# Expert weights in 2 MB pieces with 16 KB rows, and one more buffer for the first pair of experts, in a decoder block on one core

## The chip, the cores and the metric

The kernel runs on one core of a Trainium2 chip. The metric is the device time of one execution in microseconds (us); lower is better. The engines are named as the profile names them: PE is TensorE (PEld its weight loads), DVE is VectorE, ACT is ScalarE, POOL is GpSimd, SP is SyncE. SPq and ACTq are the queues in which SP and ACT issue DMAs.

## What is computed

One decoder block on 256 tokens of width 1024, all in float32. A mixer part (retention and pooling, merged by gates) comes first; then 32 experts, of which each token uses 4; then a per-layer embedding and a last norm. The change is about the experts:

```python
def swiglu_clamped(gu):
    gate, up = gu[..., :D_FF], gu[..., D_FF:]
    gate = jnp.minimum(gate, SWIGLU_LIMIT)
    up = jnp.clip(up, -SWIGLU_LIMIT, SWIGLU_LIMIT)
    return (up + 1.0) * (gate * jax.nn.sigmoid(gate * SWIGLU_ALPHA))
...
logits = xt @ w_router + b_router              # top 4 of 32, softmax over the 4
act = swiglu_clamped(xblk @ w_gate_up[e] + b_gate_up[e])   # w_gate_up[e]: 1024 x 2048
y  += slot_w * (act @ w_down[e] + b_down[e])               # w_down[e]: 1024 x 1024
```

Each expert has 8 MB of gate and up weights and 4 MB of down weights, 384 MB for the 32. All experts are computed, for up to 64 tokens each; more tokens for one expert would take an extra path (`more_pairs`), which is not entered for these inputs.

## The kernel before

**Stages.** The mixer (`column_block`, `project` and what surrounds them, L587 to L712) multiplies with weights split in a high and a low part: ACT writes w_hi (L957), DVE writes w_lo (L1201). Then come the router (L723 to L741), sixteen pairs of experts (`pair_steps` on PE, L850, and on DVE, L1435), the per-layer gate (L908 to L912) and the store (L507 to L511).

**A pair.** Two experts run side by side in TensorE: each takes 64 of its 128 columns, so a matmul of one expert lies beside that of the other. `gather` (L744) multiplies the normalised tokens xn, as stationary operand, with a one-hot matrix; DVE scales the result by the norm's gain into hg (`read_gather`, L1405). `up_bias` (L567) puts the biases in PSUM. `gate_up` (L765) goes through 8 blocks of 128 weight rows, with 4 column blocks of 512 for each expert. DVE clamps (L1413, L1414), ACT takes the sigmoid (L1075), DVE multiplies (L1418, L1422), and `act_to_width` (L774) transposes the result on TensorE (L780). `down` (L783) multiplies with w_down, and `scatter` (L802) adds the output to the tokens' rows, through DVE (L1433). In between TensorE does the previous pair's scatter and the next pair's gather. Pair 8 has extra work (`route_rest`, `project_ple`, `output_bias`, L811 to L848), which uses w_proj, 1 MB, loaded by ACT (L1048) before the first pair.

**The weights' way.** SP issues every weight load on one queue, in an order written out by hand (L453 to L484). Weights lie in a ring of 12 slots of 1 MB (8 KB for each of 128 partitions). A gate and up piece is one block of 128 rows of one expert: each partition gets one row, 8 KB in a piece. A down piece is two blocks of 128 rows: each partition gets two rows of 4 KB that lie 512 KB apart in memory. Pieces alternate between the two experts, so a pair has 24. A slot is free once the last matmul that reads it has counted up `used` (L762), and SP waits for that before each load (L483). TensorE waits for a piece of both experts before it starts on a block (`expert_ready`, L364). In gather and gate_up, row k*128 + p of a weight matrix goes with partition p of block k, and so does element k*128 + p of a token.

**Before the first pair.** The ring's upper six slots hold w_hi and w_lo of the mixer until its end: w_hi in slots 6 to 8, w_lo in 9 to 11. Loads of pair 0 start while the mixer still runs, into slots as they come free (`load_early`, L446) and into five buffers that the mixer has left (`extra_places`, L330), so 17 pieces can be there before TensorE starts on the pair. These five buffers are used once.

**Order on the other queues.** ACT issues the two bias rows of the next pair (`load_bias`, L1051), 8 KB each, into one partition each. DVE and ACT follow TensorE by semaphores that count (`chunk_used`, `gate_ready`, `act_ready`). At the start SP loads x, the norm gains and the positions (L407 to L412); TensorE transposes gains and positions (L581, L583), DVE copies them (L1187, L1188), and the first scaled columns of x wait for that.

The wait that the ring works by:

```python
with sp.Fori(1, PAIRS) as pair:
    for c in range(PER_PAIR):
        sp.wait_ge(used, PER_PAIR * pair + c - SLOTS + 1)
        load_expert(first, pair, c, 2 * pair + c % 2)
```

## Time and profile before

| | |
|---|---|
| median of 3 runs | 1279.01 us (1278.15 to 1279.05) |
| profiled execution, first to last instruction (span) | 1279.1 us |
| mean granted TensorE clock of that execution | 0.969 |
| TensorE, weight loads, DVE, ACT, POOL busy | 94%, 47%, 30%, 16%, 1% |
| moved by DMA | 456.61 MB, 357 GB/s over the span |
| chain that ended last | PE 74%, DMA 15%, DVE 9%, issue 1% |

### The profile page before, as it was taken

What the parts mean: (1) busy time and instruction counts of PE and PEld (TensorE: products, weight loads), DVE (VectorE), ACT (ScalarE), POOL (GpSimd) and SP (SyncE); (2) the same over time, 40 slices, a digit from 0 to 9 for tenths busy, and PEclk for the clock granted to TensorE, in tenths of its full rate; (3) what the DMA queues carried; (4) which work ended last, traced back from release to release, by engine and by line L of the source; (5) the groups of instructions that cost most, each with busy time, mean ns of one, the idle gap of its engine ahead of it and who ended that gap; (6) DMA issues with size and microseconds to landing.
All of it is one profiled execution on the core that took longest, in us unless ns stands there. A gap on an engine that the chain in (4) does not pass through costs nothing.

```text
span 1279.1 us, 14339 instructions
## 1 busy us (share of the span) xinstructions
PE 1204.3 (94%) x5402; PEld 596.9 (47%) x5403; DVE 383.0 (30%) x586; ACT 202.2 (16%) x266; POOL 8.2 (1%) x19
## 2 busy tenths in 40 slices
PE   7999999999999999998989999999999989989987
PEld 6888888864343434343333434334434333324235
DVE  6955656532030303122120303212303030303036
ACT  5354444320000100000000000000000000001024
POOL 0000000000000000000000000000000000000000
PEclk9999999989999999999998999899999999999998
DMA  9754355779999999999999999789999999999970
GB/s 363 261 182 156 135 197 190 281 301 361 397 414 420 416 418 418 417 419 415 420 415 421 414 421 414 326 354 421 413 422 414 422 414 421 415 419 416 417 303 33
DMA packets 98918, 456.61 MB, mean 357 GB/s; under 512 B 8282, under 2 KB 9732, under 8 KB 65956
## 3 DMA queue, kind: packets, MB, share of 16 engines
q1 hardware_dynamic: 96616, 452.00, 88.0%
q10 hardware_dynamic: 2268, 4.14, 0.9%
q8 instruction: 23, 0.38, 0.1%
q14 instruction: 11, 0.09, 0.0%
HBM read 455.06 MB, written 1.05 MB: 357 GB/s over the span
## 4 chain that ended last, share of the span: by engine, by line
PE 74%; DMA 15%; DVE 9%; issue 1%; SPq 0%; ACT 0%; DVEq 0%; POOLq 0%; POOL 0%
PE ps L517 73%; DMA ring<-in_w_gate_up 15%; DVE B L1422 2%; DVE x L1433 2%; DVE B L1413 2%; DVE B L1418 2%; DVE B L1414 2%; PE ps L524 1%; DMA x<-in_x 0%; SPq L444 0%; ACT B L1084 0%; DVE over_xn L1210 0%; DVE x L1338 0%; DVEq L1430 0%; DVE w_lo L1201 0%
## 5 line engine op out<-in xcount | busy, mean ns | idle before, releaser
L517 PE MATMUL ps<-ring,B 128*64 128x512 f32 x3032 | 688.0, 611 | 23.5 <-DMA ring<-in_w_gate_up 21.8
L517 PEld LDWEIGHTS ps<-ring,B 128*64 128x64 f32 x3032 | 223.0, 140 | 473.8 <-issue 469.7
L1413 DVE TENSOR_SCALAR B<-ps 128x1024 f32<-128x1024 f32 x16 | 19.6, 1225 | 676.8 <-PE ps L517 676.8
L1201 DVE TENSOR_TENSOR w_lo<-ring,w_hi 128x1024 fp32r<-128x1024 f32 x88 | 105.8, 1223 | 72.5 <-ACT w_hi L957 70.2
L517 PE MATMUL ps<-w_hi,over_hT 128*128 128x512 f32 x288 | 114.6, 398 | 2.6 <-DVE w_lo L1201 2.5
L517 PE MATMUL ps<-w_hi,over_xn 128*128 128x512 f32 x288 | 113.3, 393 | 0.0
L1075 ACT ACTIVATE B<-B 128x1024 f32<-128x1024 f32 x16 | 16.9, 1057 | 577.8 <-DVE B L1413 577.8
L957 ACT CAST w_hi<-ring 128x1024 fp32r<-128x1024 f32 x88 | 91.2, 1054 | 105.5 <-PE ps L517 105.2
L517 PE MATMUL ps<-w_lo,over_hT 128*128 128x512 f32 x256 | 101.0, 394 | 0.0
L517 PE MATMUL ps<-B 128*128 128x512 f32 (+3 forms) x280 | 91.8, 490 | 1.9 <-ACT B L1084 1.2
L517 PE MATMUL ps<-B,xn 128*128 128x128 f32 x512 | 65.6, 290 | 14.6 <-DVE x L1433 14.6
L517 PEld LDWEIGHTS ps<-B,xn 128*128 128x128 f32 x512 | 62.6, 203 | 20.0 <-issue 19.0
L517 PE MATMUL ps<-B,const 2*128 2x512 f32 (+3 forms) x136 | 66.9, 633 | 1.1 <-DVE x L1456 1.1
L517 PEld LDWEIGHTS ps<-B 128*128 128x128 f32 (+2 forms) x280 | 42.0, 184 | 50.9 <-issue 49.6
L517 PEld LDWEIGHTS ps<-w_hi,over_hT 128*128 128x128 f32 x288 | 55.0, 191 | 14.6 <-issue 2.9
L1084 ACT COPY B<-ps 128x1024 f32<-128x1024 f32 x16 | 16.2, 1012 | 285.7 <-PE ps L517 285.7
L517 PEld LDWEIGHTS ps<-w_hi,over_xn 128*128 128x128 f32 x288 | 54.9, 191 | 11.7
L517 PEld LDWEIGHTS ps<-w_lo,over_hT 128*128 128x128 f32 x256 | 48.9, 191 | 9.9
L1433 DVE TENSOR_TENSOR x<-x,ps 128x512 f32<-128x512 f32 x64 | 44.0, 688 | 23.7 <-PE ps L517 16.8
L517 PE MATMUL ps<-w_hi,over_B 128*128 128x512 f32 x128 | 45.1, 391 | 0.0
L517 PEld LDWEIGHTS ps<-B,const 2*128 2x128 f32 (+2 forms) x136 | 24.6, 194 | 39.5 <-issue 38.7
L517 PE MATMUL ps<-w_lo,over_B 128*128 128x512 f32 x96 | 37.3, 389 | 0.0
(141 smaller groups left out, 461.5 us busy)
## 6 DMA issues: line engine op xcount, KB each, us to landing
ring<-in_w_gate_up SPq DMA_DIRECT2D x251, 1024.0 KB, 17.3
ring<-in_w_down SPq DMA_DIRECT2D x128, 1024.0 KB, 18.9
ring<-in_w_in SPq DMA_DIRECT2D x28, 1024.0 KB, 5.3
ring<-in_w_branch SPq DMA_DIRECT2D x8, 1024.0 KB, 6.9
ring<-in_w_out SPq DMA_DIRECT2D x4, 1024.0 KB, 5.0
B<-in_w_gate_up SPq DMA_DIRECT2D x4, 1024.0 KB, 7.5
ring<-in_w_ple_gate SPq DMA_DIRECT2D x4, 1024.0 KB, 7.8
const<-in_const ACTq DMA_DIRECT2D x1, 1640.0 KB, 9.0
```

The lines of the kernel that those rows point to most:

```text
L517: return pe.matmul(out, lhsT, rhs, start=start, stop=stop, skip_group_check=True)
L524: last = pe.transpose(ps[:, bank, kk * SEQ + i * P:kk * SEQ + (i + 1) * P], src[:, i, c * P:(c + 1) * P], ident)
L957: nc.scalar.copy(w_hi[:, p % PIECES, :], piece_of(p)).then_inc(hi_ready, 1)
L1075: nc.scalar.activation(sig, gate, ACT.Sigmoid, scale=ALPHA).then_inc(s.sig_ready, 1)
L1084: nc.scalar.copy(slot_rows, two_banks(bank)).then_inc(s.os_ready, 1)
L1201: post(ve.tensor_tensor(w_lo[:, p % PIECES, :], piece_of(p), w_hi[:, p % PIECES, :].bitcast(F32), ALU.subtract), lo_ready)
L1413: step(ve.tensor_scalar(gate, two_banks(0), LIMIT, None, ALU.min), s.gate_ready)
L1414: step(ve.tensor_scalar(up, two_banks(2), LIMIT, -LIMIT, ALU.min, ALU.max), s.up_read)
L1418: step(ve.scalar_tensor_tensor(up, up, 1.0, gate, ALU.add, ALU.mult))
L1422: step(ve.tensor_tensor(gate[:, columns], up[:, columns], sig[:, columns], ALU.mult), s.act_ready)
L1433: step(ve.tensor_tensor(z, z, ps[:, SUM_BANKS[i], :], ALU.add), s.acc_done)
```

## The change

- From pair 1 on a piece is 2 MB in two neighbouring ring slots: two neighbouring rows of w_gate_up for each partition (16 KB of consecutive memory), or four of w_down (16 KB). A pair has 12 pieces instead of 24, the ring 6 places instead of 12. Pair 0 keeps pieces of 1 MB ("fine"), from the same rows: one of the two up rows (8 KB), two of the four down rows (8 KB).
- So that weights and tokens meet, the gather reads every second column of xn as stationary operand, the transposes of the activation every fourth column of gate, and the gain for hg is loaded in that order: one more DMA of 4 KB at the start, two transposes and one copy.
- TensorE waits for 2 MB of both experts and works through two blocks (gate and up) or four (down) before it frees them.
- w_hi and w_lo of one piece lie side by side, so that one used piece of the mixer frees one slot.
- Pair 0 gets six extra buffers instead of five (B[6] is the new one); the order of its loads is new. w_proj, which goes into B[6], is loaded after pair 0 instead of before it. Pair 1's first three big pieces are issued before the last six fine pieces of pair 0.
- The weights of the per-layer gate are issued once the first and second place of the last pair's ring turn are free.

```diff
-EXTRAS = 5
...
+BIG = 2 * SLOT
+FINE_UP, FINE = 2 * KD, 3 * KD
+BIG_UP, PER_PAIR = KD, KD + KD // 2
+RING = (0, 1, 2, 4, 5, 3)
+BIGS = len(RING)
+FINE_RING = (0, 1, 2, 3, 4, 5, 8, 9, 10, 11, 6, 7)
+EXTRAS = 6
+ALL_USED = FINE + (PAIRS - 1) * PER_PAIR
...
-        ring, w_hi, w_lo = sb("ring", [P, SLOTS, SLOT], (("w_hi", pieces), ("w_lo", pieces)), MIXER_SLOTS * SLOT)
+        ring, w_split = sb("ring", [P, SLOTS, SLOT], (("w_split", [P, PIECES, 2, PIECE]),), MIXER_SLOTS * SLOT)
...
-        extra_places = (B[2][:, :], B[7][:, :], B[1][:, :], hT[:, :, :].rearrange("p k s -> p (k s)"), B[5][:, :])
...
+        extra_places = (B[2][:, :], B[1][:, :], hT[:, :, :].rearrange("p k s -> p (k s)"), B[5][:, :], B[7][:, :], B[6][:, :])
+        def is_fine(s, pair):
+            return s is first and isinstance(pair, int) and pair == 0
+        def fine_unit(f):
+            if f < SLOTS:
+                return FINE_RING[f]
+            return FINE_RING[f - SLOTS] if f >= SLOTS + EXTRAS else None
+        def fine_slot(f):
+            return extra_places[f - SLOTS] if fine_unit(f) is None else ring[:, fine_unit(f), :]
+        def fine_signal(f):
+            return extra_loaded[f - SLOTS] if fine_unit(f) is None else fine_loaded[fine_unit(f)]
+        def big_slot(q):
+            at = RING[q % BIGS]
+            return ring[:, 2 * at:2 * at + 2, :].rearrange("p a n -> p (a n)")
+        def up_weights(s, pair, h, c):
+            if is_fine(s, pair):
+                return fine_slot(2 * c + h)
+            return big_slot(2 * (c // 2) + h)[:, (c % 2) * SLOT:(c % 2 + 1) * SLOT]
+        def down_weights(s, pair, h, c):
+            if is_fine(s, pair):
+                return fine_slot(FINE_UP + 2 * (c // 2) + h)[:, (c % 2) * D:(c % 2 + 1) * D]
+            return big_slot(BIG_UP + 2 * (c // 4) + h)[:, (c % 4) * D:(c % 4 + 1) * D]
+        def blocks_of(s, pair, down):
+            if is_fine(s, pair):
+                return 2 if down else 1
+            return 4 if down else 2
+        def used_after(s, pair, down):
+            if is_fine(s, pair):
+                return FINE if down else FINE_UP
+            done = PER_PAIR if down else BIG_UP
+            return PER_PAIR * pair + done + (FINE - PER_PAIR if s is first else 0)
...
+        def big_ready(eng, s, pair, q):
+            before = 1 if s is first else 0
+            eng.wait_ge(s.loaded[RING[q % BIGS]], 32 * pair + 16 * (q // BIGS + 1) - 32 * before)
+        def expert_ready(eng, s, pair, h, c, down):
+            if is_fine(s, pair):
+                fine_ready(eng, FINE_UP + 2 * (c // 2) + h if down else 2 * c + h)
+            else:
+                big_ready(eng, s, pair, BIG_UP + 2 * (c // 4) + h if down else 2 * (c // 2) + h)
...
+            sp.dma_start(hg_rows, t["g_ffn_norm"][0].rearrange("(m q) -> m q", q=2 * P)).then_inc(vec_loaded, 16)
...
-            def load_expert(s, pair, c, e):
-                i = c // 2
-                dst = slot(s, pair, c)
-                if i < UP_CHUNKS:
-                    src = t["w_gate_up"][0, bass.ds(e, 1), i * P:(i + 1) * P, :].rearrange("e p n -> p (e n)")
+            def load_fine(f):
+                e, c = f % 2, f // 2
+                if f < FINE_UP:
+                    w = t["w_gate_up"][0, e, 2 * P * (c // 2):2 * P * (c // 2 + 1), :]
+                    w = w.rearrange("(p j) n -> p j n", j=2)[:, c % 2, :]
                 else:
-                    r = (i - UP_CHUNKS) * 2 * P
-                    src = t["w_down"][0, bass.ds(e, 1), r:r + 2 * P, :].rearrange("e (k p) n -> p (e k) n", p=P)
-                    dst = dst.rearrange("p (k n) -> p k n", k=2)
-                sp.dma_start(dst, src).then_inc(signal(s, pair, c), 16)
-            def load_early(c):
-                former = MIXER_CHUNKS - 1 - (MIXER_CHUNKS - 1 - c) % MIXER_SLOTS
+                    c -= KD
+                    w = t["w_down"][0, e, 4 * P * (c // 2):4 * P * (c // 2 + 1), :]
+                    w = w.rearrange("(p j) n -> p j n", j=4)[:, 2 * (c % 2):2 * (c % 2) + 2, :].rearrange("p j n -> p (j n)")
+                sp.dma_start(fine_slot(f), w).then_inc(fine_signal(f), 16)
+            def load_big(s, q, e):
+                if q < BIG_UP:
+                    m = q // 2
+                    w = t["w_gate_up"][0, bass.ds(e, 1), 2 * P * m:2 * P * (m + 1), :].rearrange("e (p j) n -> p (e j n)", j=2)
+                else:
+                    m = (q - BIG_UP) // 2
+                    w = t["w_down"][0, bass.ds(e, 1), 4 * P * m:4 * P * (m + 1), :].rearrange("e (p j) n -> p (e j n)", j=4)
+                sp.dma_start(big_slot(q), w).then_inc(s.loaded[RING[q % BIGS]], 16)
...
             load_early(5)
             sp.wait_ge(piece_used, PARTS * (BRANCH + 3))
-            load_expert(first, 0, 6, 0)
+            load_fine(12)
             load_early(0)
             load_early(1)
             sp.wait_ge(branch_read, 3)
-            load_expert(first, 0, 7, 1)
+            load_fine(16)
             load_early(2)
             load_early(3)
             sp.wait_ge(branch_read, 4)
             for row in range(2):
                 sp.dma_start(bias_rows_first[row:row + 1, :], t["b_gate_up"][0, row:row + 1, :]).then_inc(first.bias_loaded, 16)
+            load_fine(17)
             sp.wait_ge(mT_psum, 4)
-            load_expert(first, 0, 8, 0)
+            load_fine(13)
             load_early(4)
-            for c in range(MIXER_SLOTS + EXTRAS, PER_PAIR):
-                at = in_ring(first, 0, c)
-                if at < SLOTS:
-                    sp.wait_ge(piece_used, PARTS * MIXER_BLOCKS - PIECES + 2 * ((at - MIXER_SLOTS) // 2) + 2)
-                else:
-                    former = at - SLOTS
-                    sp.wait_ge(used, (former if former < MIXER_SLOTS else former + EXTRAS) + 1)
-                load_expert(first, 0, c, c % 2)
-                if at == SLOTS - 1:
-                    load_expert(first, 0, 10, 0)
-                    sp.wait_ge(logitT_psum, 1)
-                    load_expert(first, 0, 9, 1)
-            with sp.Fori(1, PAIRS) as pair:
-                for c in range(PER_PAIR):
-                    sp.wait_ge(used, PER_PAIR * pair + c - SLOTS + 1)
-                    load_expert(first, pair, c, 2 * pair + c % 2)
+            for f in range(6, 12):
+                load_after_piece(f)
+            load_fine(15)
+            sp.wait_ge(logitT_psum, 1)
+            load_fine(14)
+            for q in range(3):
+                sp.wait_ge(used, 2 * q + 2)
+                load_big(first, q, 2 + q % 2)
+            for f in range(SLOTS + EXTRAS, FINE):
+                sp.wait_ge(used, f - SLOTS - EXTRAS + 7)
+                load_fine(f)
+            for q in range(3, BIGS):
+                sp.wait_ge(used, SLOTS + EXTRAS + 2 * (q - 3) + 2)
+                load_big(first, q, 2 + q % 2)
+            for q in range(BIGS, PER_PAIR):
+                sp.wait_ge(used, FINE + q - BIGS + 1)
+                load_big(first, q, 2 + q % 2)
+            with sp.Fori(2, PAIRS) as pair:
+                for q in range(PER_PAIR):
+                    sp.wait_ge(used, PER_PAIR * pair + q + FINE - PER_PAIR - BIGS + 1)
+                    load_big(first, q, 2 * pair + q % 2)
...
+                    sp.wait_ge(used, ALL_USED - BIGS + at // 2 + 1)
...
+            for j in range(2):
+                pe.transpose(ps[:, 0, 48 + 4 * j:52 + 4 * j], hg_rows[:, j::2], ident[0:KD // 2, 0:KD // 2])
...
-                            last = mm(ps[:, 6 + b, c * P:(c + 1) * P], xn[:, i, k * P:(k + 1) * P],
+                            last = mm(ps[:, 6 + b, c * P:(c + 1) * P],
+                                      xn[:, i, 2 * P * (k // 2) + k % 2:2 * P * (k // 2 + 1):2],
                                       onehot[:, i, :], i == 0, i == TILES - 1)
...
             def gate_up(s, pair):
-                for i in range(UP_CHUNKS):
-                    if i % 4 == 0:
-                        pe.wait_ge(s.hg_ready, 2 * pair + 1 + i // 4)
-                    for h in range(2):
-                        expert_ready(pe, s, pair, h, i)
-                    both(s, pair, i, hg, i, [n * N for n in range(4)], 0, False, i == UP_CHUNKS - 1)
+                per = blocks_of(s, pair, False)
+                for c in range(KD):
+                    if c % 4 == 0:
+                        pe.wait_ge(s.hg_ready, 2 * pair + 1 + c // 4)
+                    if c % per == 0:
+                        for h in range(2):
+                            expert_ready(pe, s, pair, h, c, False)
+                    both(s, pair, up_weights, hg, c, 2 * D, 0, c % per == per - 1)
             def act_to_width(s, pair):
                 for half in range(2):
                     pe.wait_ge(s.act_ready, 2 * pair + half + 1)
-                    for quarter in range(4):
-                        c = 4 * half + quarter
-                        last = pe.transpose(ps[:, half, quarter * P:(quarter + 1) * P], gate[:, c * P:(c + 1) * P], ident)
+                    for j in range(4):
+                        last = pe.transpose(ps[:, half, j * P:(j + 1) * P], gate[:, half * N + j:(half + 1) * N:4], ident)
                     last.then_inc(s.act_xposed, 1)
             def down(s, pair, bank=4):
-                for i in range(DOWN_CHUNKS):
-                    if i % 2 == 0:
-                        pe.wait_ge(s.actT_ready, 2 * pair + 1 + i // 2)
-                    for h in range(2):
-                        expert_ready(pe, s, pair, h, UP_CHUNKS + i)
-                    for kk in range(2):
-                        c = 2 * i + kk
-                        both(s, pair, UP_CHUNKS + i, actT, c, [kk * D, kk * D + N], bank, c == 0, c == KD - 1)
+                per = blocks_of(s, pair, True)
+                for c in range(KD):
+                    if c % 4 == 0:
+                        pe.wait_ge(s.actT_ready, 2 * pair + 1 + c // 4)
+                    if c % per == 0:
+                        for h in range(2):
+                            expert_ready(pe, s, pair, h, c, True)
+                    both(s, pair, down_weights, actT, c, D, bank, c % per == per - 1)
...
-            e.dma_start(w_proj, t["w_ple_proj"][0].rearrange("(c p) n -> p c n", p=P)).then_inc(proj_loaded, 16)
...
+            e.dma_start(w_proj, t["w_ple_proj"][0].rearrange("(c p) n -> p c n", p=P)).then_inc(proj_loaded, 16)
             with e.Fori(1, REST_PAIR) as pair:
...
+            step(ve.tensor_copy(vecs[:, 0:5 * KD], ps[:, 0, 0:5 * KD]))
+            step(ve.tensor_copy(vecs[:, G_HG:G_HG + KD].rearrange("p (m j) -> p j m", j=2),
+                                ps[:, 0, 48:56].rearrange("p (j m) -> p j m", j=2)))
...
-                    g = vecs[:, G_FFN + 4 * b:G_FFN + 4 * b + 4]
+                    g = vecs[:, G_HG + 4 * b:G_HG + 4 * b + 4]
```

## Rows read from the trace of the kernel before

**Rows 1.** The page: busy time of the engines, DMA rate in 40 slices.

```profile
PE 1204.3 (94%) x5402; PEld 596.9 (47%) x5403; DVE 383.0 (30%) x586; ACT 202.2 (16%) x266; POOL 8.2 (1%) x19
...
GB/s 363 261 182 156 135 197 190 281 301 361 397 414 420 416 418 418 417 419 415 420 415 421 414 421 414 326 354 421 413 422 414 422 414 421 415 419 416 417 303 33
```

**Rows 2.** Chain of waits of the whole span: start us, us, what.

```profile
310.38 1.24 DVE B L1413
...
361.50 1.24 DVE B L1413
...
419.19 1.24 DVE B L1413
...
782.00 1.24 DVE B L1413
...
858.54 1.24 DVE B L1413
...
914.55 1.24 DVE B L1413
```

**Rows 3.** Line L1413, all its instructions.

```profile
L1413 DVE TENSOR_SCALAR B<-ps x16: 1224/1225/1225, 310.4 to 1215.8; 128x1024 f32<-128x1024 f32 x16
```

**Rows 4.** Chain of waits between 590 and 665 us: start us, us, what.

```profile
599.39 1.24 DVE B L1413
...
637.15 19.25 DMA ring<-in_w_gate_up
...
656.53 3.68 PE ps L517 x16
...
660.23 1.24 DVE B L1413
```

**Rows 5.** Timeline of PE, 573 to 600 and 606 to 636: start us, us.

```profile
590.71 3.65 PE L517 MATMUL ps<-ring,B 128*64 128x512 f32 x16 [1.32 <-DMA ring<-in_w_gate_up]
595.69 3.65 PE L517 MATMUL ps<-ring,B 128*64 128x512 f32 x16 [1.33 <-DMA ring<-in_w_gate_up]
...
610.11 13.95 PE L517 MATMUL ps<-ring,B 128*64 128x512 f32 x64
624.00 3.70 PE L517 MATMUL ps<-B,const 2*128 2x512 f32 x8
627.62 8.78 PE L517 MATMUL ps<-ring,B 128*64 128x512 f32 x32
```

**Rows 6.** Four stretches: us, busy time of each engine, PEclk, DMA share, GB/s.

```profile
27.00:30.00 3.00, 3.00 (x15) 2.49 (x14) 3.00 (x3) 2.81 (x4) 0.00 (x0) 1.00 1.05 387
...
281.00:286.00 5.00, 4.15 (x23) 1.70 (x23) 3.39 (x10) 0.00 (x0) 0.00 (x0) 1.00 0.00 0
...
572.00:588.00 16.00, 16.00 (x78) 5.37 (x76) 0.00 (x0) 0.00 (x0) 0.00 (x0) 1.00 1.01 422
592.00:608.00 16.00, 12.84 (x60) 6.18 (x57) 7.94 (x10) 2.23 (x3) 0.00 (x0) 1.00 1.02 408
```

**Rows 7.** DMA queues (packets, MB, share); issues (count, KB each, us to landing).

```profile
q10 hardware_dynamic: 2268, 4.14, 0.9%
...
const<-in_const ACTq DMA_DIRECT2D x1, 1640.0 KB, 9.0
...
B<-in_b_gate_up ACTq DMA_DIRECT2D x30, 8.0 KB
```

**Rows 8.** Line L444 on SP's queue, its one issue from 286.1 to 286.6.

```profile
DMA to landing us min/median/max: 4.9/4.9/4.9
```

**Rows 9.** A stretch of 2.5 us, columns as in rows 6.

```profile
567.50:570.00 2.50, 2.50 (x8) 0.73 (x6) 0.00 (x0) 0.00 (x0) 0.00 (x0) 0.50 1.01 419
```

**Rows 10.** Weight loads: L780, and L517 in the gather of 606 to 610.

```profile
L780 PEld LDWEIGHTS ps<-const,B x128: 138/140/144, 314.9 to 1221.3; 128*128 128x128 f32 x128
...
L517 PEld LDWEIGHTS ps<-B,xn x32: 186/192/192, 606.3 to 609.8; 128*128 128x128 f32 x32
```

**Rows 11.** Timeline, 8 to 9 us.

```profile
8.42 0.20 DVE L1187 COPY vecs<-ps 128x40 f32<-128x40 f32 x1 [1.51 <-PE ps L583]
```

102 lines of the change are left out of this document (42 added, 60 removed).

## Prediction

> **What bounds the kernel now.** I read the page first. TensorE is busy for 94% of the span, which looks like the bound, but from the ninth slice on the DMA rate stands at 414 to 422 GB/s, with one dip where slices 26 and 27 have 326 and 354 [rows 1]. A rate that flat says that something feeds at its limit. The chain in order of time tells which it is [rows 2]: the clamp at L1413 begins when the gate and up products of a pair end; I call that moment G and number the pairs from 0. G0 is 310.4, G1 361.5, G2 419.2, G8 782.0, G9 858.5, G10 914.6, and the sixteenth, G15, is 1215.8 [rows 2, 3]. From G2 to G8 a pair takes (782.0 - 419.2) / 6 = 60.5 us, and the one between 599.39 and 660.23 takes 60.84 [rows 4]. Its chain says why: a piece of up weights lands at 637.15 + 19.25 = 656.40, TensorE starts on it at 656.53, and DVE follows at 660.23. In the timeline of PE the last two steps before G5 each waited for DMA, 1.32 and 1.33 us [rows 5]. Without them a pair would take 60.84 - 2.65 = 58.2 us. So the expert stage is bound by DMA, but TensorE is only 4% behind it. After G8 the extra work of pair 8 (G8 to G9 is 76.5 us) lets DMA fall idle, and the pair after it, without a wait for weights, takes 56.0.
>
> **What a larger row is worth.** A 1 MB piece is 64 KB on each of 16 DMA engines. I take the rate over stretches with a single row length [rows 6]: 387 GB/s with 2 KB rows (w_in), 408 with 4 KB (w_down), 422 with 8 KB (w_gate_up), which is 2.71, 2.57 and 2.485 us a piece. From 32 to 16 packets per engine saves 0.14 us, from 16 to 8 saves 0.085, so a packet costs about 9 to 10 ns beside its bytes. Four packets per MB should then take 2.445 us, and a 2 MB piece **4.89 us**. That a 16 KB row travels as one packet no row shows. The nearest is the constant load, 1640 KB over 128 partitions, 12.8 KB each: queue q10's 2268 packets come out exactly if each of these rows is one packet [rows 7]. The bounds of the piece: 4.97 if rows over 8 KB bring nothing, 4.82 if the packet cost went altogether (2.445 less 4 x 9 ns, doubled). I take 4.89, since the three row lengths lie on one line.
> Bytes per pair stay 24 MB. Before: 16 x 2.485 + 8 x 2.57 = 60.3, and the 60.84 leave 0.5 to 0.6 us, which I put down to the two 8 KB bias rows [rows 7]: each goes to one partition, so through one engine, at a sixteenth of 422 GB/s 0.31 us each. After: 12 x 4.89 + 0.6 = **59.3 us per pair**, 1.5 less.
> The Trainium skill, page DMA: Bandwidth & Descriptors, section Bandwidth, puts the ceiling of the fabric at 435.2 GB/s. By it 24 MB take 57.8 us, with the bias rows 58.4; the trace stays under it with 422.
>
> **What the coarser ring costs.** Let T be the landing of a pair's last gate-and-up piece.
> 1. Before, one step (four column blocks of both experts) follows: 656.40 to 660.23, so G = T + 3.83. After, TensorE waits for 2 MB of each expert and has two steps left. A step takes 13.95 / 4 = 3.49 us [rows 5]. G = **T + 7.3**. This is paid once per stretch bound by DMA, not per pair.
> 2. Down starts 610.11 - 599.39 = 10.7 after G [rows 4, 5], at T + 18.0. Its first half releases two slots at T + 24.9. The six slots after T carry the four down pieces and the next pair's first two, so the queue runs dry at T + 6 x 4.89 = T + 29.3. The seventh must be issued earlier by the latency: the piece issued to an idle queue at 286.2 landed after 4.9 us, of which 2.5 are transfer, so 2.4 [rows 8]. 24.9 + 2.4 = 27.3: **2 us of slack**.
> 3. The next gate and up start at T + 18.0 + 13.9 + 3.6 (bias) = T + 35.5. Its first double step meets the 1.2 GHz level (granted clock 0.50 from 567.5 to 570.0 [rows 9], about 30 us after G4, behind the stretch of transposes and DVE work in which TensorE was half idle): 32 records from 627.62 took 8.78 us instead of 2 x 3.49 [rows 5]. Slots free at T + 44.3, needed by T + 10 x 4.89 + 0.6 - 2.4 = T + 47.1. Slack 2.8.
> 4. TensorE alone needs 58.2, so it still waits 1.1 us per pair. DMA stays the bound, barely.
>
> **The other parts.** w_hi and w_lo interleaved, the new order of early loads and one extra buffer: the 12 ring slots and all buffers are full before the first gate and up (the rate is 0 from 281 to 286 [rows 6]), and the extra megabyte takes the place of w_proj, which moves from there to after pair 0. Nothing, in a stretch that DMA has to spare; if not, 2.5 us. Chunks of pair 1: now three big pieces go out at steps 2, 4 and 6, filling gaps that the fine ones left, and the next three wait for pieces 20, 22 and 24 of pair 0. Reckoned through by slots, pieces 6 and 7 wait for the first double step of pair 1's gate and up, which starts at 361.5 - 8 x 3.49 + 0.9 = 334.5 and frees its slots at 341.5; they land at 341.5 + 2.4 + 2 x 4.89 = 353.7, say 354.3 with w_proj among them. Needed: 362.4 - 7.2 = 355.2. No stall, but 1 us off one.
> At the start: one more small DMA before positions (0.3), two small transposes (2 x 0.25), one copy (0.20 and its gap [rows 11]), ahead of the first scaled column. **+0.9 us**; bounds 0.3 and 1.2.
> Strided operands: the gather loads every second float of xn, the transposes every fourth of gate, as stationary operands. No load in the trace is strided. The contiguous ones: 32 loads in the gather, spaced 0.11 us; 8 in the transposes at 140 ns [rows 10]. Bounds: nothing, or twice the time (a guess, as no row is near), 8 x 0.14 = 1.1 and 32 x 0.11 = 3.5, 4.6 us per pair. I take nothing, since the nearest rows are these same loads, and the number of floats stays.
> The Trainium skill, page SBUF — State Buffer, section Door 1: The DMA port swizzle, speaks against part of this: two hits are needed per 16-byte line. By it the gather (two floats per line) is free and the transposes (one) pay, and the sum below would be 3 us higher (the mild form of rival B). No run so far shows it.
>
> **The sum.** G0 311.3, G1 362.4 (TensorE's pace, +0.9). G2 = 354.3 + 59.3 + 7.3 = 420.9, later than before by 1.7. G8 = 420.9 + 6 x 59.3 = 776.7, 5.3 earlier. G9 = +76.5 = 853.2. For G10: TensorE frees its first double step 6 x 3.49 = 20.9 before G9, the last two pieces land at G9 - 20.9 + 2.4 + 9.8 = G9 - 8.7, the next pair's 59.3 later at G9 + 50.6, so G10 = G9 + 57.9 = 911.1 (before, + 56.0). G15 = 911.1 + 5 x 59.3 = 1207.6, against 1215.8. The tail follows G15, whose down pieces have landed in time in both. 1279.1 - 8.2 = 1270.9, **1271**. Span and median (1279.01) agree within 0.1, so no correction.
>
> **Rivals.**
> A. *Long rows bring nothing* (16 KB split in two, or costs by the byte). A pair takes 12 x 4.97 + 0.6 = 60.2: G2 421.9, G8 783.1, G9 859.6, G10 918.5, G15 1219.5: **1283**, slower, because G = T + 7.3 and the lost slack after pair 8 have no return. It decides from 4.95 us a piece. Against it: the line of three row lengths and the 12.8 KB rows. 12%.
> B. *TensorE reads the strided operands slowly.* It then is the bound at 58.2 + e per pair. From G0 to G15 TensorE then takes 51.1 + 7 x 58.2 + 76.5 + 56.0 + 5 x 58.2 + 15e = 882 + 15e, against 905.4 before; with the start's 0.9 it is slower from e = 1.5. e = 1.1 gives 1274, e = 3.5 or 4.6 gives 1309 to **1326**. For it: no row shows a strided load; against it: nothing but that the floats are as many. 14% for slower, 8% for the mild form, which ends with the forecast.
> C. *The queue runs dry* while down's first half holds two slots: slack 2 us. A stall of 1 us per pair gives 1283, of 0.5 us 1277. Against it: the latency is measured. 8%, most of it for half a microsecond.
> D. *DMA gains more*, 4.82 a piece, 58.4 a pair, where TensorE's 58.2 stands next: G2 420.1, G8 770.7, G9 847.2, G10 904.2, G15 1196.4: **1260**. 6%.
> The forecast itself 52%, 1266 to 1276, for pieces of 4.86 to 4.92.
>
> **How the numbers follow.** 0.2% (2.6 us) is about what a measurement of this kernel can tell from no change. Faster: the forecast, the mild form of B, D and a little of C: 0.68. Slower: A and B from e = 1.7: 0.26. Same: most of C, 0.06. The range goes from near D to A with its margin, 1262 to 1284, leaving out the strong form of B and the ends of C and D.
>
> **What would show it.** Right: G to G 59.3, up and down stretches both near 428 GB/s, 4.9 us between starts of TensorE's double steps where it waits, G about 7.3 after the landing. Wrong: a rate of 422 (A); loads over 140 ns and no wait for DMA before G (B); a rate that dips once per pair about 30 us after the last up piece (C).

## The result, and the profile after

The kernel with the change takes **1289.78 us** (median of 4 runs, 1284.06 to 1294.33), the one before 1278.58 beside it: a ratio of 1.0092, with a 95% interval of 1.0064 to 1.0121. It is slower by 11 us. The forecast was 1271, and the range ended at 1284. The profiled execution, the slowest of the four, spans 1292.5 us, 13.4 more than the profiled one before.

The page of the kernel after, in the lines that answer to [rows 1, 7]:

```profile
PE 1219.5 (94%) x5404; PEld 612.8 (47%) x5405; DVE 383.1 (30%) x587; ACT 202.0 (16%) x266; POOL 8.3 (1%) x19
...
GB/s 363 265 177 163 119 203 188 323 243 277 327 404 423 430 426 417 425 425 421 426 414 417 430 412 427 352 283 426 427 415 428 418 430 407 407 418 429 428 281 33
...
q1 hardware_dynamic: 54320, 451.99, 85.2%
q10 hardware_dynamic: 2268, 4.14, 0.9%
...
ring<-in_w_gate_up SPq DMA_DIRECT2D x120, 2048.0 KB, 13.5
```

The reader is to see that the change does what it says: SP's queue moves the same 452 MB in 54,320 packets (96,616 before), which comes out exactly if each 16 KB row is one packet and each DMA adds one small packet per engine for its semaphore. Many slices now stand at 425 to 430 GB/s where 414 to 422 stood [rows 1]. But TensorE is busy for 15 us more. The clamp, now at L1460, tells where the time went, as L1413 did in [rows 3]:

```profile
L1460 DVE TENSOR_SCALAR B<-ps x16: 1224/1225/1225, 324.4 to 1229.2; 128x1024 f32<-128x1024 f32 x16
```

G0 stands at 324.4 instead of 310.4, and G15 at 1229.2 instead of 1215.8. From G0 to G15 it is 904.8 us against 905.4. So **14.0 us are already lost at G0**, when the first pair's gate and up end, and the expert stage from G0 to G15, which was to give 9.1 us, gives 0.6. These are two questions.

**What happens before G0.** The chain of waits of the kernel after, from 247 to 300 (start us, us, what):

```profile
247.31 0.24 ACTq L1091
...
247.59 28.34 DMA B<-in_b_router
...
275.97 5.92 PE ps L559 x16
```

A DMA of 16 KB takes 28 us. It is the router's bias, issued on ACT's queue (L1092) after the router's weights (L1091), and TensorE needs both for the router's product. The timeline of PE shows the gap, of the kernel after:

```profile
265.02 1.09 PE L566 MATMUL ps<-const,x 128*128 128x128 f32 x8 [0.70 <-DVE x L1385]
275.97 5.91 PE L559 MATMUL ps<-hT,B 128*32 128x256 f32 x16 [9.86 <-DMA B<-in_b_router]
```

and of the kernel before, where the same product follows without a wait:

```profile
264.87 1.09 PE L524 MATMUL ps<-const,x 128*128 128x128 f32 x8 [0.70 <-DVE x L1338]
265.89 3.64 PE L517 MATMUL ps<-hT,B 128*32 128x256 f32 x16
```

The wait is 9.86 us, and it costs more than itself. Behind it the granted clock is lower for longer. The windows of the kernel after (us, busy time of the engines, PEclk, DMA share, GB/s):

```profile
266.00:276.00 10.00, 0.14 (x2) 0.03 (x2) 1.21 (x5) 5.03 (x7) 0.89 (x2) 0.72 0.93 365
276.00:282.00 6.00, 5.88 (x16) 2.36 (x16) 0.01 (x1) 0.00 (x0) 0.00 (x0) 0.62 0.02 8
282.00:296.00 14.00, 13.26 (x46) 8.74 (x46) 4.22 (x22) 1.82 (x3) 0.00 (x0) 0.63 0.22 75
```

and of the kernel before, over the same work:

```profile
266.00:270.00 4.00, 3.53 (x16) 1.57 (x15) 1.42 (x6) 2.91 (x6) 0.89 (x2) 1.00 1.01 422
270.00:282.00 12.00, 11.58 (x46) 8.28 (x46) 3.90 (x22) 3.79 (x5) 0.00 (x0) 0.72 0.72 298
```

The router's product takes 5.91 instead of 3.64 (2.3 more), and the work up to the first gate and up 14.0 instead of 12.4 (1.6 more; 282.45 to the chain's start of gate and up at 296.56, against 270.11 to 282.55). 9.9 + 2.3 + 1.6 = 13.8 of the 14.0 us.

Why does the bias take 28 us? The DMA issues between 244 and 260 (what, count, KB each, median us to landing), of the kernel after:

```profile
B<-in_w_router ACTq DMA_DIRECT2D x1, 128.0 KB, 25.7
...
B<-in_b_router ACTq DMA_DIRECT2D x1, 16.0 KB, 28.3
```

and of the kernel before:

```profile
B<-in_w_router ACTq DMA_DIRECT2D x1, 128.0 KB, 5.7
...
B<-in_b_router ACTq DMA_DIRECT2D x1, 16.0 KB, 9.2
```

The same bytes in the same queue, issued at 247.1 instead of 247.0, take 25.7 us instead of 5.7. The packets of the two queues (packets, MB, share; q1 is SP's, q10 ACT's) show how, from 252 to 272 in the kernel after:

```profile
q1 hardware_dynamic: 1096, 7.95, 96.9%
q10 hardware_dynamic: 1097, 0.14, 4.5%
```

and from 250 to 254 in the kernel before:

```profile
q1 hardware_dynamic: 101, 0.70, 44.9%
q10 hardware_dynamic: 1232, 0.45, 43.2%
```

After, one packet of ACT's goes for one of SP's, although SP's are 8 KB and the router's 128 bytes. Before, over a thousand go in 4 us while SP has little in flight. What differs is SP: the diff puts the fine load of piece 17 in front of SP's wait for mT_psum, at 246.50, with piece 13 behind it at 247.12. Before, one piece was issued then, at 246.98, and the next at 248.45. The theory (call it Q): the router's weights are 1024 rows of 128 bytes, and each engine alternates between the packets of the two queues, so each small row stands behind a packet of 8 KB as long as SP's queue is full. As an estimate, 1024 rows are 64 for each of 16 engines, and 64 packets of 8 KB at 0.31 us are 20 us, which is what the 25.7 are over the 5.7. How fast the router's rows land is set by what SP has in flight, not by their 144 KB.

**What happens in the expert stage.** The windows of the kernel after, two stretches of pair 2 with up weights under way throughout:

```profile
456.00:468.00 12.00, 12.00 (x42) 3.91 (x40) 0.00 (x0) 1.01 (x1) 0.00 (x0) 0.87 1.01 421
470.00:482.00 12.00, 12.00 (x58) 3.93 (x56) 0.00 (x0) 0.00 (x0) 0.00 (x0) 1.00 1.00 427
```

The spacing of the 2 MB landings, read from the ring's semaphores, is 4.89 us wherever nothing comes between, as forecast. The chain of pair 4:

```profile
534.87 13.51 DMA ring<-in_w_gate_up
...
548.51 7.11 PE ps L559 x32
...
555.64 1.23 DVE B L1460
```

T is 548.38 and G is 555.64: T + 7.3, as forecast. From G1 on, most pairs take 58.7 to 59.9. But behind G3, G10 and G12 the starts of L1460 stand 60.3, 60.5 and 61.5 apart, and these are three of the five pairs (3, 7, 10, 12, 13) in which the gather ran at the lower clock. Timeline of PE after G2 and after G12:

```profile
441.20 1.48 PE L825 MATMUL ps<-const,B 128*128 128x128 f32 x8 [0.72 <-DVE B L1469]
443.63 4.03 PE L559 MATMUL ps<-B,xn 128*128 128x128 f32 x32 [0.95 <-DVE x L1480]
...
1055.54 5.49 PE L559 MATMUL ps<-B,xn 128*128 128x128 f32 x32 [0.98 <-DVE x L1480]
1060.97 11.38 PE L559 MATMUL ps<-ring,B 128*64 128x512 f32 x52
```

and the windows behind G12:

```profile
1055.00:1059.00 4.00, 3.46 (x17) 3.46 (x18) 2.21 (x4) 0.18 (x1) 0.00 (x0) 0.57 0.99 422
1066.00:1072.00 6.00, 6.00 (x30) 2.01 (x28) 0.00 (x0) 0.00 (x0) 0.00 (x0) 1.00 0.85 314
```

Behind G12 the gather takes 1.5 us more than behind G2, down starts 12.4 instead of 10.9 after G, its first half frees two slots 1.5 us later, and the DMA rate falls to 314 GB/s right where the forecast placed its slack of 2 us: the seventh piece lands 7.68 us after the sixth (1070.64 and 1078.32) instead of 4.89.

### The profile page after: what moved, and what is told of

The parts are those of the page before. It is cut to its first block, busy times and chain, and to the rows that moved or that the text cites. A ratio compares the mean times of both kernels' runs of the same rounds, so it can differ in the third digit from the quotient of the medians.

```text
span 1292.5 us, 13525 instructions
## 1 busy us (share of the span) xinstructions
PE 1219.5 (94%) x5404; PEld 612.8 (47%) x5405; DVE 383.1 (30%) x587; ACT 202.0 (16%) x266; POOL 8.3 (1%) x19
## 3 DMA queue, kind: packets, MB, share of 16 engines
q1 hardware_dynamic: 54320, 451.99, 85.2%
q10 hardware_dynamic: 2268, 4.14, 0.9%
## 4 chain that ended last, share of the span: by engine, by line
PE 74%; DMA 14%; DVE 9%; issue 1%; ACT 1%; SPq 0%; DVEq 0%; POOLq 0%; POOL 0%; ACTq 0%
PE ps L559 74%; DMA ring<-in_w_gate_up 12%; DMA B<-in_b_router 2%; DVE B L1469 2%; DVE x L1480 2%; DVE B L1460 2%; DVE B L1465 2%; DVE B L1461 2%; PE ps L566 1%; SPq L475 0%; DMA x<-in_x 0%; DVE over_xn L1257 0%; ACT B L1128 0%; ACT over_hT L1010 0%; PE ps L825 0%
## 5 line engine op out<-in xcount | busy, mean ns | idle before, releaser
L1460 DVE TENSOR_SCALAR B<-ps 128x1024 f32<-128x1024 f32 x16 | 19.6, 1225 | 667.5 <-PE ps L559 667.5
L559 PE MATMUL ps<-w_split,over_hT 128*128 128x512 f32 x544 | 173.8, 396 | 2.9 <-DVE w_split L1248 2.7
L1248 DVE TENSOR_TENSOR w_split<-ring,w_split 128x1024 fp32r<-128x1024 f32 x88 | 105.9, 1223 | 72.2 <-ACT w_split L1002 70.3
L559 PEld LDWEIGHTS ps<-w_split,over_hT 128*128 128x128 f32 x544 | 103.0, 191 | 24.7 <-issue 3.1
L559 PE MATMUL ps<-w_split,over_xn 128*128 128x512 f32 x288 | 113.1, 393 | 0.0
L1002 ACT CAST w_split<-ring 128x1024 fp32r<-128x1024 f32 x88 | 91.2, 1054 | 105.3 <-PE ps L559 105.0
L559 PE MATMUL ps<-w_split,over_B 128*128 128x512 f32 x224 | 61.6, 390 | 0.0
L559 PEld LDWEIGHTS ps<-w_split,over_xn 128*128 128x128 f32 x288 | 54.9, 190 | 11.6
L559 PEld LDWEIGHTS ps<-w_split,over_B 128*128 128x128 f32 x224 | 41.8, 188 | 8.5
L1456 DVE TENSOR_TENSOR B<-ps,vecs 128x512 f32<-128x512 f32 x32 | 22.1, 691 | 44.7 <-PE ps L559 44.1
L825 PE MATMUL ps<-const,B 128*128 128x128 f32 x128 | 23.6, 310 | 11.5 <-DVE B L1469 11.5
```

The costliest lines, as they stand in the source:

```text
L559: return pe.matmul(out, lhsT, rhs, start=start, stop=stop, skip_group_check=True)
L825: last = pe.transpose(ps[:, half, j * P:(j + 1) * P], gate[:, half * N + j:(half + 1) * N:4], ident)
L1002: nc.scalar.copy(w_split[:, p % PIECES, 0, :], piece_of(p)).then_inc(hi_ready, 1)
L1248: post(ve.tensor_tensor(w_split[:, p % PIECES, 1, :], piece_of(p), w_split[:, p % PIECES, 0, :].bitcast(F32), ALU.subtract), lo_ready)
L1456: step(ve.tensor_tensor(hg[:, 4 * b:4 * b + 4, :], bank_cols(6 + b, 4), across(g, P), ALU.mult), s.hg_ready)
L1460: step(ve.tensor_scalar(gate, two_banks(0), LIMIT, None, ALU.min), s.gate_ready)
```

## The experiments

All times are medians, and the ratios are to the kernel before, run beside each of them; its median was 1278.2 or 1278.3 each time. Experiments 6 and 10 are the same kernel, run twice; both stand under heading 6. The distances from G to G that no fence shows are read from the starts of the clamp in each trace, and the stretches of low clock from its clock records.

**1 and 2. Is it piece 17?** Both are the kernel after with one step moved. The first issues piece 17 last of the early pieces:

```diff
-            load_fine(17)
             sp.wait_ge(mT_psum, 4)
...
             load_fine(14)
+            load_fine(17)
```

> The changed kernel, with fine piece 17 issued behind piece 14 instead of before the wait for the transposed mixer output. Theory Q (the 128-byte rows of w_router and b_router in ACT's queue take turns with SP's packets, and piece 17, issued in the same microsecond, keeps SP's queue full under them): the router weights land about 6 us after issue instead of 25.7, b_router about 9 instead of 28.3, the router no longer waits, G0 comes at 311 instead of 324.4, and the time falls by 13 us, to 1277. Rival R (the coarser ring and the strided operands cost it, and the late router only shifts work that then has less to wait for): G0 falls, but the time by under 5 us, to 1285 or more.

The second keeps piece 17 where the change put it, and moves the two router loads from ACT to SP, right in front of it:

```diff
+            sp.dma_start(w_router, t["w_router"][0].rearrange("(k p) n -> p k n", p=P)).then_inc(router_loaded, 16)
+            sp.dma_start(b_router, t["b_router"].to_broadcast([P, N_EXPERTS])).then_inc(router_loaded, 16)
             load_fine(17)
```

> The changed kernel, with the two router loads issued by SP, right before fine piece 17, instead of by ACT. Bytes and pieces stay, only the order on the engines' queues is new. Theory Q: w_router and b_router land within 6 us of their issue, G0 comes at 311 to 313, time 1276 to 1279. Rival (the engines had simply more bytes to move before the router, or many small rows are slow on their own wherever they are queued): w_router still lands over 15 us after issue, and G0 stays near 324.

Measured: 1272.81 us (1271.29 to 1276.71), ratio 0.9950 (0.9932 to 0.9968), and 1274.21 us (1272.51 to 1277.95), ratio 0.9973 (0.9960 to 0.9987). The DMA issues between 244 and 260, of the first:

```profile
B<-in_w_router ACTq DMA_DIRECT2D x1, 128.0 KB, 5.8
...
B<-in_b_router ACTq DMA_DIRECT2D x1, 16.0 KB, 18.3
```

and of the second:

```profile
B<-in_w_router SPq DMA_DIRECT2D x1, 128.0 KB, 2.6
...
B<-in_b_router SPq DMA_DIRECT2D x1, 16.0 KB, 6.4
```

In the first TensorE goes from the transposes to the router's product without a wait, and the clamp is at its old place:

```profile
L1460 DVE TENSOR_SCALAR B<-ps x16: 1223/1225/1226, 310.1 to 1213.5; 128x1024 f32<-128x1024 f32 x16
```

The second has G0 at 309.9. In one queue, ahead of the big packets, the small rows take 2.6 us although the same pieces follow; beside them, in a queue of their own, 25.7. One expectation was missed: in the first the bias takes 18.3 us and not 9, and lands at 265.4, where TensorE starts on the product at 265.5. The same order gave 7.0, 9.3 and 12.6 us in experiments 4, 5 and 8, so this cure can work with little to spare, while the second has room. Both times came out below the 1277 and 1276 to 1279 that were expected. So the place of one line holds all 14 us of G0, and 16 or 17 us of the time with what follows. With it mended the change is faster than before by 4 to 5 us, and 1.8 or 3.2 us off the forecast.

**3. Does it work the other way round?** The kernel before, with the 1 MB of w_proj taken from ACT's queue and issued on SP in front of its wait for mT_psum, so that SP, as in the kernel after, has 1 MB more in flight:

```diff
+            sp.dma_start(w_proj, t["w_ple_proj"][0].rearrange("(c p) n -> p c n", p=P)).then_inc(proj_loaded, 16)
             sp.wait_ge(mT_psum, 4)
```

> The kernel before, with w_proj (1 MB) issued by SP before its wait for the transposed mixer output instead of by ACT behind the router loads: the same bytes, now in SP's queue while the small router rows are in ACT's. Theory Q: the router loads land 20 us or more after issue as in the changed kernel, G0 moves from 310.4 to 320 or later, and the kernel before gets 8 to 14 us slower, near 1290, or less if the stage bound by DMA swallows part of it (DMA fell idle before 286, so little is swallowed). Rival: what delays the router is the extra buffer or the 8 KB rows of the changed kernel; then this one stays within 2 us of 1279.

Measured: 1287.41 us (1284.8 to 1290.45), ratio 1.0069 (1.0046 to 1.0091). The chain of waits:

```profile
247.78 26.25 DMA B<-in_b_router
...
274.08 5.44 PE ps L518 x16
```

and the issues:

```profile
B<-in_w_router ACTq DMA_DIRECT2D x1, 128.0 KB, 20.6
...
B<-in_b_router ACTq DMA_DIRECT2D x1, 16.0 KB, 26.3
```

The old kernel gets the same stall with none of the change in it. G0 moves from 310.4 to 318.9, a little short of the 320 expected, and from G0 to G15 next to nothing changes (905.1 against 905.4). Theory Q holds in both directions. By the Trainium skill, page DMA: Bandwidth & Descriptors, section Queues, rings and completion order, an engine goes round robin between its queues by packets. The traces agree: 1096 packets of one queue and 1097 of the other in 20 us, and the router's weights take 5.7 us beside a queue that runs dry, 20.6 and 25.7 beside a full one, 2.6 ahead of the pieces in the same one.

**4. The bias rows over 16 engines.** The prediction put 0.6 us a pair on two 8 KB rows, each on one engine. The first kernel above, with each row viewed as 16 runs:

```diff
-                    e.dma_start(bias_rows[h:h + 1, :], t["b_gate_up"][0, bass.ds(ex, 1), :]).then_inc(s.bias_loaded, 16)
+                    e.dma_start(bias_rows[h:h + 1, :].rearrange("o (a n) -> o a n", a=16),
+                                t["b_gate_up"][0, bass.ds(ex, 1), :].rearrange("o (a n) -> o a n", a=16)).then_inc(s.bias_loaded, 16)
```

> As the first kernel of this call, and each bias row is loaded as 16 runs of 512 bytes instead of one of 8 KB. Theory E (each 8 KB bias row occupies one DMA engine for 0.31 us, 0.6 us per pair, and that engine sets when pieces land): the gaps between landings that are 0.6 us over 4.89 vanish, the distance from first to last engine of a landing stays small, a pair bound by DMA takes 58.8 us instead of 59.4, and the time falls by 4 to 7 us against the first kernel, less where TensorE (58.2 to 58.5) is the bound. Rival (the 0.6 us has another cause, such as the loop's turn on SP): no change.

Measured: 1275.12 us (1272.68 to 1281.18), ratio 0.9977 (0.9961 to 0.9993). The page still shows

```profile
q10 hardware_dynamic: 2268, 4.14, 0.9%
```

as in [rows 7]: the runs lie side by side in memory, and the row went as one packet again. The edit changed no packet, and the run says nothing of the theory that it was to test. It is of use as a repeat of the first: 1272.8 and 1275.1 show how far the same DMAs scatter from one run to the next.

**5. What the long rows give, and what the coarse ring costs.** The first kernel, with each 2 MB piece as two DMAs of 8 KB rows and nothing else changed (the awaited counts double):

```diff
-                sp.dma_start(big_slot(q), w).then_inc(s.loaded[RING[q % BIGS]], 16)
+                for half in range(2):
+                    part = slice(half * SLOT, (half + 1) * SLOT)
+                    sp.dma_start(big_slot(q)[:, part], w[:, part]).then_inc(s.loaded[RING[q % BIGS]], 16)
```

> The first kernel of the former call (changed kernel, piece 17 late), but each 2 MB piece is loaded by two DMAs of 1 MB with rows of 8 KB. Ring, places, waits and order stay: row length alone. Theory L (the gain is 9 ns per packet saved, 4.89 us for 2 MB with 16 KB rows, 4.97 with 8 KB): landings of 2 MB 4.97 apart, a pair bound by DMA 60.3 instead of 59.4, time 8 to 12 us above that kernel's 1272.8, so 1281 to 1285, slower than before. Rival (the coarse ring's gain comes from fewer DMAs and waits, not from the rows): within 2 us of 1273.

Measured: 1284.36 us (1283.89 to 1293.03), ratio 1.0048 (1.0025 to 1.0072). The windows of this kernel:

```profile
456.00:468.00 12.00, 12.00 (x58) 3.92 (x56) 0.00 (x0) 0.00 (x0) 0.00 (x0) 1.00 1.01 422
470.00:482.00 12.00, 10.38 (x50) 3.71 (x48) 0.00 (x0) 0.00 (x0) 0.00 (x0) 1.00 1.01 421
```

and of the first kernel:

```profile
456.00:468.00 12.00, 12.00 (x56) 4.00 (x54) 0.00 (x0) 0.00 (x0) 0.00 (x0) 0.95 1.01 430
470.00:482.00 12.00, 10.07 (x50) 3.57 (x48) 0.00 (x0) 0.00 (x0) 0.00 (x0) 1.00 1.01 431
```

421 to 422 GB/s become 430 to 431. This is rival A made real: it was worked out as 1283. So within this ring the long rows give 9 to 12 us (1284.4 less 1275.1 or 1272.8). Without them the changed kernel is 6 us slower than the kernel before, but that one still has 4 KB rows in w_down. At equal rows the difference is 15 us, as experiment 6 shows.

**6. The rows without the ring.** If rows are what pays, the fine ring can have part of them: w_gate_up's 1 MB pieces have 8 KB rows already, and only w_down goes in 4 KB rows [rows 6]. The kernel before, with two consecutive rows of w_down per partition, and the transposes of gate taken at every second float to match:

```diff
-                    src = t["w_down"][0, bass.ds(e, 1), r:r + 2 * P, :].rearrange("e (k p) n -> p (e k) n", p=P)
-                    dst = dst.rearrange("p (k n) -> p k n", k=2)
+                    src = t["w_down"][0, bass.ds(e, 1), r:r + 2 * P, :].rearrange("e (p k) n -> p (e k n)", k=2)
...
-                        last = pe.transpose(ps[:, half, quarter * P:(quarter + 1) * P], gate[:, c * P:(c + 1) * P], ident)
+                        first_row = 2 * P * (c // 2) + c % 2
+                        last = pe.transpose(ps[:, half, quarter * P:(quarter + 1) * P],
+                                            gate[:, first_row:2 * P * (c // 2 + 1):2], ident)
```

> The kernel before with one edit: a down piece takes two neighbouring rows of w_down for each partition, 8 KB of consecutive memory instead of two of 4 KB, and the transposes read every second column. Twelve-slot ring, 1 MB pieces and early order stay. Theory L: a down piece lands 2.49 instead of 2.56 us after the one before it, a pair takes 60.25 instead of 60.85, over some 11 pairs bound by DMA 6 to 7 us less: 1271 to 1272, as good as the changed kernel with its order mended, since G stays at 3.8 us behind the landing instead of 7.3. Rival (strided transposes cost as much as they save): 1277 or more.

Measured: 1269.49 us (1267.58 to 1272.03), ratio 0.9927 (0.9907 to 0.9948). It was run once more, on another chip:

> The kernel before with 8 KB down rows and nothing else, once more, on the same chip as the one above. If 1269.5 holds, 1268 to 1271 and 0.7% under before; if that was one chip's luck, within 0.3% of before.

Measured: 1269.07 us (1268.94 to 1270.32), ratio 0.9926 (0.9908 to 0.9945). The page of this run, and its clamp:

```profile
GB/s 363 263 176 156 148 195 173 279 330 344 379 421 422 422 422 422 422 422 422 422 422 422 422 422 421 365 333 422 422 422 422 422 422 422 422 422 422 421 331 34
...
L1414 DVE TENSOR_SCALAR B<-ps x16: 1224/1225/1226, 310.3 to 1206.6; 128x1024 f32<-128x1024 f32 x16
```

The rate has no dips left: 421 or 422 in the slices of the expert stage, but for those of pair 8 and the two ends. A pair takes 60.3, which is 24 x 2.485 + 0.6 = 60.2 by the prediction's own figures, and G0 to G15 takes 896.3 (905.4 before). Of these 9.1 us, 1.4 lie in pair 8, which no weights bound. **This is the fastest version** but for experiment 9, which only adds to it and is 0.6 us lower; it is 9 us under the kernel before and 3 to 6 under the change with piece 17 mended.

With 8 KB rows everywhere the fine ring takes 1269.1 to 1269.5 and the changed kernel 1284.4 (experiment 5). So the coarser ring, with the rest of the change around it (the extra buffer alone is 2.7 us, experiment 7), costs about 15 us, and the 16 KB rows give back 9 to 12 of them. What the ring alone costs was not separated. In experiment 10 too the clock was low in the gather of three pairs (4, 7 and 13), and the distances behind them are 60.2 and 60.3 like the others: the fine ring has room for it.

**7. The extra buffer alone.** The kernel before with six extra buffers, and w_proj's load behind pair 0:

```diff
-EXTRAS = 5
+EXTRAS = 6
...
                     load_expert(first, 0, 9, 1)
+                    load_expert(first, 0, 11, 1)
```

> The kernel before with the sixth extra buffer alone: piece 11 of pair 0 goes into it, issued last of the early loads, and w_proj is loaded after pair 0. My reckoning: 1 MB more is there before the first gate and up, but w_proj's 1 MB now lies in the stretch bound by DMA, so the two cancel: within 1.5 us of before, 1277 to 1280. Rival (one more buffer gives TensorE a lead that lasts): 2 to 3 us less, 1276.

Measured: 1282.23 us (1280.15 to 1283.75), ratio 1.0021 (1.0001 to 1.0041). A miss: I had it within 1.5 us of before, and it is 2.7 us over it by the ratio, 4.0 by the medians. The windows of this kernel:

```profile
288.00:300.00 12.00, 12.00 (x60) 4.00 (x58) 0.00 (x0) 0.00 (x0) 0.00 (x0) 1.00 1.02 413
300.00:312.00 12.00, 12.00 (x67) 5.19 (x64) 1.89 (x2) 0.66 (x1) 0.00 (x0) 1.00 0.61 232
```

and of the kernel before:

```profile
300.00:312.00 12.00, 12.00 (x64) 5.00 (x61) 1.59 (x2) 0.36 (x1) 0.00 (x0) 1.00 0.87 313
```

The sixth buffer fills while DMA is idle anyway. But the ring takes its next piece only when TensorE has passed one more extra piece, so DMA idles longer between 300 and 312 (232 against 313 GB/s), and w_proj's megabyte, 2.5 us, now lies in the stretch that DMA bounds: the distance from G2 to G3 is 60.3 instead of 58.8, from G1 to G2 58.7 instead of 57.7.

**8 and 9. The bias rows in one DMA of two rows**, which puts them on two engines, in the first kernel and in the fastest one (the awaited count follows):

```diff
+                if s is first:
+                    e.dma_start(bias_rows, t["b_gate_up"][0, bass.ds(experts[0], 2), :]).then_inc(s.bias_loaded, 16)
+                    return
```

> The first kernel of the former call with both bias rows of a pair in one DMA of two rows, so that they go to two partitions in one DMA, instead of two DMAs of one row. (Cutting each row in 16 runs had left queue q10's packets at 2268, so it changed nothing.) Theory E (two single rows both fall on the same engine, 0.31 us each, and two rows of one DMA on two engines): the extra gap in a pair shrinks from 0.6 to 0.8 us by 0.3, a pair takes 59.1 instead of 59.4, time about 3 us below 1272.8. Rival (the gap has another cause): no change.

> The kernel before with 8 KB down rows (twelve-slot ring, 1 MB pieces) and the pair's two bias rows in one DMA. In that kernel DMA, not TensorE, sets the pair (60.25 against 57.7 where no piece is waited for), so the 0.31 us that the former call's last kernel took out of the gap between landings should show in the time here: pairs of 59.9 and 2 to 4 us below the same kernel without this edit, so about 1266. Rival (the bias rows' gap never sets a landing that TensorE waits for): within 1 us of it.

Measured: 1275.49 us (1273.64 to 1281.04), ratio 0.9974 (0.9950 to 0.9998), and 1268.43 us (1267.35 to 1271.89), ratio 0.9924 (0.9905 to 0.9942). Both expectations of a gain are missed: no gain shows in the first, and 0.6 to 1.1 us instead of 2 to 4 in the second, inside the scatter. The rows do run side by side now: in the packet records of experiment 8 two packets of 8 KB start at 604.84 and 604.96 and take 0.31 us each, where experiment 1 has them at 607.10 and 608.64. But less comes of it than I took. In experiment 1 the long landing distance of a pair is 5.70 us and the next one 4.72, together 0.63 over two of 4.89 or 4.90. In experiment 8 they are 5.34 and 4.89, together 0.45. So a pair gains 0.2 us and not 0.3, and the pairs take 58.7 to 59.8 and one 60.8. In the fine ring the long distance stays at 3.1 us (2.49 for the others) and the pair at 60.3, although the rows run side by side there too; why stays open.

## Why the prediction was wrong

- **The bound, and the piece.** Held. DMA bounds the stage; the 2 MB piece takes 4.89 us, a 16 KB row is one packet, and experiment 5 shows that the row length carries the gain.
- **G = T + 7.3.** Held: 7.26 (555.64 less 548.38).
- **59.3 us per pair.** Held where nothing stalls: 59.3 or 59.4 in eight of the fifteen stretches of experiment 1. Beside the twelve pieces there are 0.6 us, as taken: one landing distance of 5.70 and behind it one of 4.72.
- **"The other parts ... Nothing": this step failed.** It judged the new order of early loads by one question, whether the buffers are full before they are needed, and answered it rightly: DMA had idle time until 286. It did not ask who else had a transfer in flight at the moment at which piece 17 was now issued. It followed SP's queue and not ACT's, where the router's 144 KB in rows of 128 bytes began to go out 0.6 us later (246.50 and 247.14). The step was put at nothing, and it costs 14.0 us of G0 and turns a gain of 4 to 5 into a loss of 11 (experiments 1 to 3). No rival had it.
- **The slack of 2 us.** Named in the right place, but the sum took the gather at its usual pace, with the lower clock only 30 us behind G [rows 9]. In five pairs after the change the low stretch also came about 7 us after G, in the gather (granted clock 0.57 from 1055 to 1059), and took 1.5 of the 2 us. Part of the slack was not there either: the sixteen engines complete one piece over 1.97 us in the semaphore records, so the first of them run dry before T + 29.3. This is **rival C** in part, 0.9 to 2.1 us in three pairs. A slow gather alone does not decide it: in experiment 1 only one of five such pairs lost time (pair 2, 61.5), the others took 59.3 or 59.4. The last double step is exposed in the same way: in experiment 1 the low clock fell on it once, it took 8.80 us instead of 7.11 (chain, 1204.55), and that pair 62.0. In experiment 5 it fell there three times (61.6, 62.0 and 62.0), but the pairs behind the first two took 58.5 and 58.6, so this is lost for good only at the end. What puts the low clock at one place in one pair and at another in the next stays open; the kernel before has it in the gather behind one of G1 to G14 (pair 7), experiment 1 in five, and experiment 10 in three. A coarse ring that frees its slots in halves would tell how much this is worth; it was not tried.
- **The start, +0.9 us.** Nothing of it reached G0. The first scaled column starts at 10.24 instead of 9.80, but G0 stands at 309.9 to 310.5 in experiments 1, 2, 4 and 8, against 310.4 before and 311.3 forecast.
- **Pair 0.** G0 to G1 took 52.9 where 51.1 was forecast, because a low stretch of the clock lay about 24 us behind G0. It did in every profile with the new ring, but also in experiments 3, 9 and 10, which keep the old one, while 6 and 7 have 51.2 and 51.1; 6 and 10 are the same kernel. So this 1.8 us can come without the change, and whether the change makes it more frequent is open. G1 to G2, where w_proj's 2.5 us were put at 0.6, took 59.4 where 58.5 was forecast.
- **Rival B, slow strided operands.** Seen in the loads, hardly in the time. The transposes' weight loads, every fourth float, take 212 instead of 140 ns [rows 10]:

```profile
L825 PEld LDWEIGHTS ps<-const,B x128: 195/212/220, 328.9 to 1234.8; 128*128 128x128 f32 x128
```

  Yet eight transposes take 1.48 instead of 1.39 us: a weight load overlaps the product ahead of it. The gather of 32, every second float, takes 4.03 instead of 3.83. That is 0.3 us a pair on TensorE, while it waits 1 us for weights. Experiment 10, with every second float in the transposes, has loads of 209 ns and 1.47 for the eight, so every second float was hardly cheaper to load than every fourth. The step "I take nothing" was nearly right in time and wrong in what I named as its sign, loads over 140 ns. By the Trainium skill, page SBUF — State Buffer, section Door 1: The DMA port swizzle, the gather should have been free and the transposes should have paid; the trace shows 0.2 us for the one and 0.1 for the other, and the measurement decides.
- **Rival A** came out in experiment 5 near its price, 1284 for 1283. It was not the reason here. **Rival D** did not occur: 430 GB/s, 4.89 a piece.
- **The extra buffer: "Nothing ... if not, 2.5 us".** In the old kernel alone the second bound was nearer (experiment 7: ratio 1.0021, which is 2.7 us, with an interval from 0.1 to 5.2; the medians differ by 4.0).

Taken together: forecast 1271, with piece 17 mended 1272.8, 1274.2, 1275.1 and 1275.5 in experiments 1, 2, 4 and 8. One step taken as nothing was 14 us and more. For the rest the total is off by only 2 to 4 us, but that is partly luck. From G0 to G15 the forecast was 896.3 us, and the profiles of experiments 1, 2, 4 and 8 have 903.4, 901.8, 901.2 and 900.9, so the stage gave 2.0 to 4.5 us of the 9.1 forecast. G0 came 0.8 to 1.5 us earlier than forecast, and what follows G15 took 60.6 to 61.5 us instead of the 63.3 of the profiled execution before, which the forecast carried over. In that execution the clock was low in two more stretches behind G15 than in experiment 2, which has 60.6. These two made up for 2.7 to 4.2 of the 4.6 to 7.1 us by which the stage fell short.

## What to carry to other kernels

Before an issue is moved to an earlier place, list every transfer that is in flight there, on all queues, with its row size and who waits for it: a load in rows of 128 bytes beside a full queue of large packets took 25.7 us instead of 5.7. Put such loads ahead of the large ones in the same queue, or issue them while the others are dry. And where longer rows are wanted, look first for the tensor whose rows are still short: here w_down's 4 KB rows made 8 KB gave 9 us in the fine ring, while 16 KB rows for all, in pieces twice as large, gave 9 to 12 us more and the coarser ring around them took about 15. Compare such versions at equal rows, or the one gain is counted against the wrong cost.

## What the runs showed of the hardware that was not expected

- Two queues share the engines packet for packet and not by bytes: in 20 us 1097 packets of 0.14 MB in all went beside 1096 of 7.95 MB. Beside a queue with little in flight 1232 went in 4 us.
- A gap of TensorE costs more than its length: 9.9 us of waiting were followed by 3.9 us more for the same work, at a granted clock of 0.62 and 0.63 where 1.00 and 0.72 had been.
- The packet cost of 9 to 11 ns a row holds from 2 KB to 16 KB rows: 2.71, 2.57, 2.485 and 2.445 us per MB.
- A row of one partition that is written as 16 adjacent runs still travels as one packet (experiment 4: 2268 packets in ACT's queue, as before).
- Weight loads of the transposes with a stride of two or four floats take half as long again, 209 and 212 against 140 ns, and the eight transposes show 0.1 us of it.
